# A PEER block and an MoE layer on one core: output projection, first queries, first search and gathers put into one block, token rows loaded once

## The reference, cut to what matters

```
h = h + concatenate([ya, yb, yc]) @ w_out
n = rmsnorm(h, g_ffn)
q = (n @ w_q).reshape(t, 8, 256);  q1, q2 = halves of q
s1, s2 = q1 and q2 against 128 sub-keys each, per head
v1, i1 = top_k(s1, 16);  v2, i2 = top_k(s2, 16)
vals, ci = top_k(v1 + v2 of all 256 pairs, 16)
idx = e1 * 128 + e2;  gates = softmax(vals)        # 8 heads x 16 = 128 experts a token
act = gelu(n . expert_u[idx]) * gates
h = h + sum over the 128 experts of act * expert_v[idx]
```

## Time and profile before

| | |
|---|---|
| median of 3 runs | 3154.69 us (3153.26 to 3154.82) |
| the profiled execution's own time | 3160.97 us |
| its span, first to last instruction | 3159.1 us |
| busy: PE, DVE, POOL, ACT | 81%, 44%, 23%, 22% |
| gathers (L1758) | 512, first at 233.7 us, last at 1682.5 us |
| mean granted TensorE clock | 0.90 |

### The profile page before, as it was taken

How to read it: one execution, slowest core, us unless ns; L and a number is a source line. 1 busy time by engine, 2 the same in 40 slices (tenths; PEclk the granted TensorE clock), 3 DMA queues, 4 the chain that set the end, 5 groups by cost and what they waited for, 6 DMA issues and landing times. The chain is left out here.

```text
span 3159.1 us, 33335 instructions
## 1 busy us (share of the span) xinstructions
PE 2549.0 (81%) x12787; PEld 1192.6 (38%) x12787; DVE 1382.4 (44%) x3088; ACT 690.8 (22%) x1946; POOL 713.5 (23%) x632
## 2 busy tenths in 40 slices
PE   8997885675556858766788987869999999899994
PEld 4454332341111414322345766733333333333331
DVE  3945666667778686566544143151111111111113
ACT  1212322322223232353223152110101000000001
POOL 0202343334444434544431010200000000000002
PEclk9998997897777989778999998979999999999997
DMA  5229999999999999999996472189999999999996
GB/s 191 104 72 368 400 377 370 389 400 421 420 416 415 416 401 411 381 407 415 421 421 265 140 233 70 54 347 414 410 414 404 415 413 411 405 420 411 406 414 261
DMA packets 152577, 1099.44 MB, mean 348 GB/s; under 512 B 17792, under 2 KB 24448, under 8 KB 54656
## 3 DMA queue, kind: packets, MB, share of 16 engines
q0 software_dynamic: 79232, 556.31, 43.6%
q1 hardware_dynamic: 64896, 529.97, 42.2%
q10 hardware_dynamic: 8288, 11.02, 1.0%
HBM read 1065.77 MB, written 31.46 MB: 347 GB/s over the span
## 5 line engine op out<-in xcount | busy, mean ns | idle before, releaser
L1996 PE MATMUL banks<-arena,spare 128*64 128x512 f32 x2048 | 645.5, 765 | 429.3 <-ACT spare L1937 422.1
L1867 DVE SCALAR_TENSOR_TENSOR arena<-arena 128x1024 f32<-128x1024 f32 x512 | 626.3, 1227 | 443.0 <-DMA arena<-in_expert_uv,picked 442.0
L1758 POOL DMA_INDIRECT arena<-in_expert_uv,picked x512 | 584.4, 1141 | 921.5 <-PE banks L1996 713.5
L2249 PE MATMUL banks<-arena,aT 128*64 128x512 f32 (+1 forms) x4032 | 613.5, 504 | 26.2 <-DMA arena<-in_expert_w 25.5
L1996 PEld LDWEIGHTS banks<-arena,spare 128*64 128x64 f32 x2048 | 149.3, 162 | 840.9 <-ACT spare L1937 599.3
L2249 PEld LDWEIGHTS banks<-arena,aT 128*64 128x64 f32 (+1 forms) x4032 | 213.7, 125 | 400.4 <-issue 356.9
L2573 DVE TENSOR_SCALAR aT<-banks 128x512 f32<-128x512 f32 (+1 forms) x49 | 30.2, 616 | 627.0 <-PE banks L2267 627.0
L2261 PE MATMUL banks<-arena,aT 128*64 128x512 f32 (+1 forms) x2016 | 303.9, 501 | 0.4
L2189 POOL DMA_INDIRECT picked<-moe_rows,extra x32 | 30.5, 954 | 1016.8 <-PE banks L2235 933.7
L1926 ACT ACTIVATE spare<-spare 128x2 f32<-128x2 f32 x256 | 52.0, 203 | 901.0 <-DVE arena L1867 900.9
L1154 PE MATMUL banks<-aT,arena 128*128 128x256 f32 x768 | 181.5, 395 | 1.7 <-DVE aT L1119 1.7
(11 more groups left out here) (316 smaller groups left out, 2099.7 us busy)
## 6 DMA issues: line engine op xcount, KB each, us to landing
arena<-in_expert_w SPq DMA_DIRECT2D x192, 2048.0 KB, 36.3
arena<-in_mid_w SPq DMA_DIRECT2D x58, 1024.0 KB, 9.0
arena<-in_w_q SPq DMA_DIRECT2D x8, 2048.0 KB, 13.2
expert_rows<-aT ACTq DMA_DIRECT2D x70, 128.0 KB, 9.0
arena<-in_expert_uv,picked POOLq DMA_INDIRECT x512, 12.4
expert_rows<-h SPq DMA_DIRECT2D x8, 1024.0 KB, 14.8
arena<-in_w_in SPq DMA_DIRECT2D x3, 2048.0 KB, 13.8
arena<-in_w_out SPq DMA_DIRECT2D x2, 2048.0 KB, 7.8
```

The source lines that it names most:

```text
L1758: eng.indirect_dma_start(places[place_of[n]], None, uv_rows, bass.IndirectOffsetOnAxis(ap=eidx[:, n:n + 1], axis=0))\
L1867: nc.vector.scalar_tensor_tensor(out=u, in0=u, scalar=1.0, in1=twice[tt % 2][:, n % 2, :], op0=ALU.mult, op1=ALU.mult, accum_out=dots[:, k ...
L1996: mm = nc.tensor.matmul(bank[g * HALF:(g + 1) * HALF, sum_bank[tt] + half, :], diag[:, (n + g) % NDIAG, :], places[place_of[n + g]][:, D + ...
L2249: mm = nc.tensor.matmul(bank[tile, b_, 0:width], xT[:, c % 2 * 4 + k, r0:r0 + nrows], w[:, k * D + lo:k * D + lo + width], start=c % 2 == ...
```

## The change

The mixer's block and the PEER block become one. The bodies of the mixer's engines move into functions `mixer_sync`, `mixer_scalar`, `mixer_vector`, `mixer_tensor` and `mixer_gpsimd` without a change of their own. The projection's steps are written out: turns of tile 0 between the two products of tile 1; queries and scores of groups 0 and 1 before the products of tile 2; the search of head 0 between the scaling of tile 1 and the adds of tile 2. The sums of tiles 0 to 3 go to banks (3, 7), (0, 1), (2, 3), (0, 1), the turns to (4, 5), (0, 1), (2, 3), (0, 1). Before the gathers the queries of groups 2 to 7 are computed; those of groups 8 to 15 move to pairs 1 to 8, and the wide ones to every second pair from 11 on. Head 1's search moves from `START` to `REST`. The ring's places are used in another order, starting with 4. Tile 0's rows are copied from `rows` in SBUF by ScalarE and no longer stored; the rows of tiles 1 to 3 are loaded to partitions 0 to 63 only, and ScalarE copies them to 64 to 127 at pairs 56, 120 and 184.

```diff
 
             def sync(self, sp):
...
+            def product(self, eng, i, n):
+                if i == 0:
+                    wait_chunk(eng, self.c0 + n)
+                if i == 3:
+                    eng.wait_ge(dve_done, self.dv["out", 1, 1])
+                for k in range(KD):
+                    mm = nc.tensor.matmul(bank[:, self.sums[i][n], :], self.src[:, k, i * P:(i + 1) * P],
+                                          chunk_view(self.c0 + n)[:, k, :], start=k == 0, stop=k == KD - 1)
+                mm.then_inc(pe_done, 1)
+
+            def turn(self, eng, i):
+                eng.wait_ge(dve_done, self.dv["scale", i])
                 for n in range(2):
-                    wait_chunk(eng, self.c0 + n)
-                for i in range(NT + 1):
-                    if i < NT:
-                        for w in ready[i]:
-                            eng.wait_ge(*w)
-                        for n in range(2):
-                            if i >= 2:
-                                eng.wait_ge(dve_done, self.dv["add", i - 2, n])
...
+        def mixer_sync(sp):
+            load_chunk(sp, 2)
...
-                projection.scalar(eng)
...
-                projection.vector(eng)
...
-                projection.tensor(eng, [first, others, [], []])
...
-        START = [("head", 0, 0), ("head", 0, 1), ("gates", 0, 0, 2)]
+        START = [("head", 0, 0), ("gates", 0, 0, 1)]
...
-            batches_of = [((0, 2), (2, 4), (4, 6), (6, 8)), ((0, 2), (2, 4), (4, 8)), ((0, 4), (4, 8)), ((0, 4), (4, 8))][tt]
+            batches_of = [((0, 1), (1, 2), (2, 4), (4, 6), (6, 8)), ((0, 2), (2, 4), (4, 8)), ((0, 4), (4, 8)), ((0, 4), (4, 8))][tt]
...
+            return min(ALL_STEPS, -(-ALL_STEPS * n // (HEAD_EVERY * (N_HEADS - 1))))
         top = sem("top_steps")
...
-        EARLY, LATE, TURN = (0, 1, 2, 3, 4, 5), (6, 7, 8, 2, 3, 4, 0, 1), 98
+        EARLY, LATE, TURN = (4, 0, 1, 2, 3, 5), (6, 7, 8, 1, 2, 3, 4, 0), 98
...
+        AHEAD = HH // 2
+
         def q_at(g):
-            return 2 + 5 * g // 2
+            return 11 + 2 * g
         q_pairs = {}
+        for g in range(AHEAD, HH):
+            for i, what in enumerate(("first_q", "copy_first_q", "first_s", "copy_first_s")):
+                q_pairs.setdefault(g - AHEAD + 1 + i, []).append((what, g))
         for g in range(HH):
...
-        def load_twice(sp, tt):
+        def load_once(sp, tt):
             for g in range(2):
-                for lo in range(2):
-                    sp.dma_start(twice[tt % 2][lo * HALF:(lo + 1) * HALF, g, :],
-                                 xn_dram[tt * P + g * HALF:tt * P + (g + 1) * HALF, :]).then_inc(rows_twice[tt % 2], 16)
+                sp.dma_start(twice[tt % 2][0:HALF, g, :], xn_dram[tt * P + g * HALF:tt * P + (g + 1) * HALF, :])\
+                  .then_inc(rows_once[tt % 2], 16)
+
+        def copy_first_rows(g, lo):
+            nc.scalar.activation(twice[0][lo * HALF:(lo + 1) * HALF, g, :], rows[g * HALF:(g + 1) * HALF, 0, :], ACT.Copy)\
+              .then_inc(rows_twice, 1)
+
+        def copy_twice(eng, tt):
+            eng.wait_ge(rows_once[tt % 2], 32 * ((tt + 1) // 2))
+            nc.scalar.activation(twice[tt % 2][HALF:P, :, :], twice[tt % 2][0:HALF, :, :], ACT.Copy).then_inc(rows_twice, 1)
...
-                    load_twice(sp, 2)
+                    load_once(sp, 2)
...
+                    load_once(sp, 3)
                 if unit == ("in2", s, 3):
...
             def _(sp):
-                sp.dma_start(xn_dram.rearrange("(t p) d -> p t d", p=P), rows[:, :, :]).then_inc(rows_out, 16)
-                sp.wait_ge(rows_out, 16)
-                load_twice(sp, 0)
+                mixer_sync(sp)
+                sp.wait_ge(dve_done, projection.dv["scale", NT - 1])
+                sp.dma_start(xn_dram[P:S, :].rearrange("(t p) d -> p t d", p=P), rows[:, 1:NT, :]).then_inc(rows_out, 16)
                 for c, groups in ((C_Q + 2, 4), (C_Q + 3, 8), (C_Q2, 12), (C_Q2 + 1, 16), (C_Q2 + 2, 20), (C_Q2 + 3, 24)):
                     sp.wait_ge(q_done, groups)
                     load_chunk(sp, c)
+                sp.wait_ge(rows_out, 16)
                 sp.wait_ge(row_added, second_use + 1)
-                load_twice(sp, 1)
+                load_once(sp, 1)
                 mid_sp(sp)
 
             @block.gpsimd
             def _(eng):
+                mixer_gpsimd(eng)
...
+                        elif place_of[n] in (2, 3, 5):
+                            eng.wait_ge(pe_done, projection.pe["p", 3, 1])
                         elif place_of[n] in (6, 7):
                             eng.wait_ge(q_done, 2 * HH)
...
+                mixer_vector(eng)
                 nc.vector.tensor_tensor(ident2, ident[:, 0:HALF], ident[:, HALF:P], ALU.add).then_inc(ident2_ok, 1)
-                for _ in search(START):
+                opening = search(START)
+                eng.wait_ge(row_in, projection.row_at)
+                projection.add(eng, 0, 0)
+                projection.add(eng, 0, 1)
+                projection.scale(eng, 0)
+                projection.add(eng, 1, 0)
+                projection.out(eng, 0)
+                projection.add(eng, 1, 1)
+                projection.scale(eng, 1)
+                for _ in range(length(START[0])):
+                    next(opening)
+                projection.add(eng, 2, 0)
+                projection.out(eng, 1)
+                projection.add(eng, 2, 1)
+                projection.scale(eng, 2)
+                projection.add(eng, 3, 0)
+                projection.out(eng, 2)
+                projection.add(eng, 3, 1)
+                projection.scale(eng, 3)
+                for _ in opening:
                     pass
+                projection.out(eng, 3)
                 ahead = search(REST)
                 between = Aside(chain(kv_dve(eng), mid_vector(eng, 0)))
                 for tt in range(NT):
-                    eng.wait_ge(rows_twice[tt % 2], 64 * (tt // 2 + 1))
+                    eng.wait_ge(rows_twice, tt + 4)
                     for k in range(GK):
...
+                mixer_scalar(eng)
+                projection.square(eng, 0)
+                projection.square(eng, 1)
+                for g in range(2):
+                    copy_q(g, g, P)
+                for g in range(2):
+                    copy_first(g)
+                exponentials(batches[0])
+                projection.square(eng, 2)
+                projection.square(eng, 3)
+                for g in range(2, AHEAD + 1):
+                    if g < AHEAD:
                         copy_q(g, g, P)
-                    if g:
-                        eng.wait_ge(s_done, g)
-                        nc.scalar.activation(first[:, g - 1, :], bank[:, 6 + (g - 1) % 2, 0:P], ACT.Copy).then_inc(s_copied, 1)
-                    if g == 6:
-                        exponentials(batches[0])
+                    if g > 2:
+                        copy_first(g - 1)
+                    if g == 2:
+                        eng.wait_ge(pe_done, projection.pe["p", 3, 1])
+                    if g < 6:
...
+                    if pair % (GK // PAIR) == GK // PAIR - 8 and tt + 1 < NT:
+                        copy_twice(eng, tt + 1)
...
+                def first_queries(g):
+                    if g % 4 == 0:
+                        wait_chunk(eng, C_Q + g // 4)
+                    if g >= 2:
+                        eng.wait_ge(q_copied, g - 1)
+                    queries(g, g, range(KD), 0, P).then_inc(q_done, 1)
+
+                mixer_tensor(eng)
+                eng.wait_ge(act_done, ac["silu", 0, TA - 1])
+                eng.wait_ge(dve_done, dv["u2", 0])
+                eng.wait_ge(pool_done, mixer_po["out", TB - 1])
+                projection.product(eng, 0, 0)
+                projection.product(eng, 0, 1)
+                eng.wait_ge(act_done, ac["silu", 1, TA - 1])
+                eng.wait_ge(dve_done, dv["u2", 1])
+                projection.product(eng, 1, 0)
+                projection.turn(eng, 0)
+                projection.product(eng, 1, 1)
                 eng.wait_ge(late_in, keys_at)
-                for g in range(HH + 1):
-                    if g < HH:
-                        if g % 4 == 0:
-                            wait_chunk(eng, C_Q + g // 4)
-                        if g >= 2:
-                            eng.wait_ge(q_copied, g - 1)
-                        queries(g, g, range(KD), 0, P).then_inc(q_done, 1)
-                    if g:
+                eng.wait_ge(dve_done, projection.dv["out", 0, 1])
+                for g in range(2):
+                    first_queries(g)
+                for g in range(2):
+                    scored(g, g, 1)
+                projection.product(eng, 2, 0)
+                projection.turn(eng, 1)
+                projection.product(eng, 2, 1)
+                projection.product(eng, 3, 0)
+                projection.turn(eng, 2)
+                projection.product(eng, 3, 1)
+                for g in range(2, AHEAD + 1):
```

(54 more changed lines are left out.)

445 lines of the change are left out of this document (192 added, 253 removed).

## The result

The changed kernel takes 3127.03 us (median of 4 runs, 3124.08 to 3131.37), the kernel before beside it 3153.98 (4 runs, 3153.19 to 3154.82): a ratio of 0.9913, with an interval of 0.9902 to 0.9925, so 27 us less. The forecast was 18.6 less.

The account below looks back on a forecast made before the run. It took the expert stage's gather ring to be bound by DMA bandwidth. Terms -18.1 - 1 - 4 - 1.5 + 4 + 2 = -18.6 us took the median 3154.69 to 3136.1 us; range 3122 to 3152, the forecast's own stretch 3127 to 3146.

Parts of the forecast that it names:

- the new start: Before the expert gathers: gather 0 at 194.0 us, 39.7 earlier, and gather 6 at 234.6 against 269.07.
- more than forecast: Rival 3: no stall at pair 16, no query loss, more from bytes and pair 48; -29.6 us, 3125; chance 0.12.
- the stall at pair 16: Early ring: ScalarE waits for gates of heads 2 and 3 until gather 36 has landed; +4 us (0 to 9).
- What the start is worth: Gap before gather 6: 42.8 us of DMA work still to do, so -18.1 us, and -1 for less refilling.
- Rival 4: Early gathers bring nothing, only the shorter query loop counts: 3139 us; already in the count, no chance of its own.
- less one gather: Stall at pair 16: DMA dry from DVE over ScalarE and TensorE to a new issue, minus gather 37; +4 us.
- Fewer bytes: Tiles 1 to 3 load 0.5 MB less each where the DMA is full: -4 us (0 to 7).
- The rule of the ports: Partitions 0 to 63 reach only 8 of 16 ports, so halving tile loads gains nothing; sum 4 us higher.
- The stall at pair 48: ScalarE's 26.7 us wait for memory rows behind tile 1's loads; they land sooner: -1.5 us (0 to -3.5).
- The packed queries: Eight queries in pairs 1 to 8, wide ones every two pairs from 11: +2 us over 34 pairs (0 to 8).
- The slower rival: Rival 2: TensorE falls to its low clock in pairs 11 to 45; 3175 us at half share; chance 0.09.
- The tail: Work after the expert ring, TensorE busy 1089 of the last 1210 us: shifts one to one with the ring's end.

Follow-up runs that it names:

- split-gates kernel: Changed kernel with tile 0's gates of heads 2 and 3 made in batches of their own, one head at a time: 3116.71 us, ratio 0.9880 to the kernel before.
- all queries first: Changed kernel with all 16 first queries ahead of the ring again, none in pairs 1 to 8: 3147.37 us, ratio 0.9974 to the kernel before.
- second trace: The changed kernel run again without any edit: 3127.60 us, ratio 0.9914 to the kernel before.

## Why the prediction was right, and where its size was off

The sign, the new start and the time's place in the range held. The size did not: 27 us less in place of 18.6, at the very edge of the forecast's own stretch (3127 to 3146), towards the rival "more than forecast", and reached another way than that rival had it. That it came out no further off is in part luck: the start was undersized by 10 us or more, and the stall at pair 16, undersized by 5, took half of that back. Point by point:

**The new start** was right to 3 us: gather 0 at 193.5 (194.0), gather 1 at 205.8 (206.4), gather 3 at 213.6 (214.2), gather 6 at 231.8 (234.6). VectorE's search came ahead of the adds of tile 2, as forecast.

**What the start is worth** is the step that failed. I counted the DMA work that the gap had carried, 42.8 us of it, as work that the ring must then carry at full price, so that a lead of 34.5 us at gather 6 was worth 18.1, plus 1 for slack. That rests on the reading "the 16 DMA engines are busy for all of the time". The share was full, but the rate was not: the same rows say 349 and 398 GB/s, and from gather 6 to 95 it was 383 at 0.98. The split-gates kernel, which has no stall, shows what that is worth, by the DMA queues of these stretches. Before, 95.65 MB went between gathers 6 and 95, 4.19 of it weights and other plain loads, in 249.84 us: 2.81 us a gather. With split gates it was 102.33 MB, 10.83 of it plain loads, in 252.06: 2.83 us a gather, and 406 GB/s at a share of 1.01. At 383 GB/s 102.33 MB would have taken 267. The changed kernel and the one with all queries first, both with the stall, say it less strongly: 103.23 MB in 262.84 us against 96.25 in 255.84. So some 7 MB more weights in the ring cost 2 to 7 us in place of 17. In the changed kernel itself the lead is still 31.2 at gather 36, just before its stall (28.6 in its second trace). The start is thus worth 29 to 31 us in the traces, and not 19. The medians say the same: the split-gates kernel is 39.0 us under the kernel before, of which 6 to 8.5 are the loads of tiles 1 to 3, so 30 to 33 are left.

That this room is used up in the changed kernel is shown: weights loaded again cost their full price now, 20 of the 22.6 us. That it was there in the ring of before is read from the traces alone; no run adds loads to that ring. That the gap mattered by gather 6 more than by gather 0 is shown by the kernel with all queries first (19.8 us for 29 us of gather 6), but so is that the early gathers count: held back, they cost 10.4, where I had put gather 0 at 2.5 and said that the rest was in the count already. Rival 4 was wrong for this reason. Tile 0's rows from SBUF are worth 11 by themselves.

Why the ring of before ran at 383 is open. It isn't TensorE: with 47 us of its work gone the rate was 385. The kernel with all queries first speaks for the plain loads themselves: with as few of them as before, the changed kernel's own code runs at 366 GB/s and a share of 0.94 ahead of its stall, and at 401 behind it. The other traces of the changed kernel and its variants, with more plain loads, show 398 to 415 in the stretches without a stall. A ring that takes some 2.8 us a gather by itself, and in which plain loads fill what the gathers leave, would look like this; what sets those 2.8 us no run shows. It isn't the whole of it: in 430:470 the kernel before moves 359 against 405 in the changed one. It may in part be the one execution that was profiled: another execution of nearly the same ring, the kernel before with rows loaded once, shows 390.

**The stall at pair 16** was found with its place and its chain, and undersized: +4, with 9 as the upper end. The lead falls from 31.2 to 22.1 over it, ScalarE waits 8.7 us and the DMA's share in 311.85:358.16 is 0.82, so 8.3 us of 46.31. Taking it away gave 10.9. The way from the last dot (330.88) over ScalarE and TensorE to the new issue (337.42) took 6.5 us, as the sum had it. What failed is "less one gather", by which the gather under way would cover 2.5 us of it. In steps of 2 us from 328 the DMA's share is 0.97, 0.49, 0.03, 0.00, 0.00, 0.51, 0.95: it ran dry from about 331, with gather 37 covering next to nothing, until about 339, and the 1.6 us or so from the issue to the new data had no term at all. No weights filled the hole.

**Fewer bytes** gave 6.0 to 8.5 us together with what they save at pair 48, against -4 (0 to 7) and -1.5. The estimate by the rate of the first such loads, 7, was the nearer of the two that I had, and I took the other. By bytes alone 1.5 MB at 411 GB/s is 3.7. Tile 2's load has no stall beside it: over gathers 128 to 144 the lead grows from 30.3 to 34.2 with rows loaded once and from 25.9 to 26.0 with them loaded twice, for 0.5 MB, whose bytes make 1.3. The rule of the ports that I set against it (the Trainium skill, SBUF — State Buffer, "Door 1: The DMA port swizzle") would have left no gain from the removed half, and the runs show one. It would also have given a gain from spreading the rest; none shows, though 2 to 4 us of it would be within the noise. This says nothing of the rule where such loads stand alone.

**The stall at pair 48** shrank by 3 us of wait (26.7 to 23.8), and not by the earlier start: with rows loaded twice it is 27.1, and in the kernel before with rows loaded once 23.7. What that is worth by itself no run shows. Taken away altogether, the stall is worth 5 to 6 more by the times, with the noise nearly as large, and 6 by the lead behind it.

**The packed queries** were put at +2 (0 to 8). TensorE was 89% busy, where I forecast over 90%, and the DMA ran at 411 GB/s beside it; no loss shows, though no run takes this packing alone. The slower rival needed a low clock there, and the granted clock was 1.00.

**The tail** took the shift one to one, 37.6 to 35.6 us.

In sum the traces give about -31 for the start, +9 for the stall at pair 16, and -14 for bytes and pair 48 together (the lead grows from 22.1 at gather 38 to 30.2 at gather 112, 34.2 at 144 and 37.6 at 336, in steps at the tiles' loads). That makes 36, and the spans differ by 35.6; the last term is what is left over, and not a measurement of its own. The medians give 27. The difference is mostly the profiled execution of before, 6 to 7 us above its medians; the second trace of the changed kernel ends its ring with a lead of 33.2.

## What to carry to other kernels

A DMA share of 0.98 doesn't say that nothing more fits in: read the GB/s beside it, against the best stretch of the same access pattern, before work that moves into that stretch is charged at full price. When a search or a softmax is moved into a ring whose order is written out by hand, check each product of it against the step that consumes it; here one batch that was done behind dot 36, and needed at dot 32, cost 10.9 of some 38 us, and a split of the batch gave them back. A load on a queue that stands behind others (the memory rows) is cheap to move up, and was worth some 5 to 6.

## What the runs showed of the hardware

The same row gathers, with 4.19 MB of plain loads among them, ran at 383 GB/s and a DMA share of 0.98 in the kernel before; with 10.83 MB among them, at 406 GB/s and 1.01 in the kernel with split gates. These 6.6 MB took 2.2 us more for the same 89 gathers (7.0 us for 7 MB in the pair with the stall). A further 8.4 MB cost 2.7 us a MB (22.6 / 8.4, of which 2.4 us are a wait for the weights).

Loads of 4 KB rows to 64 partitions inside a full ring cost more than their bytes: 1.5 MB for 6.0 to 8.5 us, a shorter stall at pair 48 included, and about 4 us of lead for the 0.5 MB of tile 2, where the bytes make 1.3. Their place in the upper or the lower partitions made no difference that shows (0.9912 and 0.9914, with some 0.2% of noise).

With six places and no new gather issued, the DMA's share fell from 0.97 in 328:330 to 0.03 in 332:334 and 0.00 in 334:336. It was at 0.51 again in the 2 us that begin 0.6 us behind the next issue at 337.42.
